# Regrouping the modulation pieces and retiming selection rounds and compressed attention in a fused two-block transformer kernel

## The chip, the cores and the metric

One core of a Trainium2 chip runs the whole program. The metric is the device time of one execution in microseconds (us). The kernel computes in float32: each weight tile and each activation is split into a high and a low part, and a product is three matmuls.

## The reference, cut to what matters

```python
mod = c @ w_ada[l] + b_ada[l]                     # 6 x 1024 values
h = rms_norm(x, g_pre_mix[l]) * (1.0 + sc1) + sh1 # uses the first two of six
proj = h @ w_in[l]
# nsa_attention: three branches of the same queries
k_cmp = compress(kc, ...); v_cmp = compress(vc, ...)   # a small MLP over blocks of 32 keys
o = g0 * o_cmp + g1 * o_slc + g2 * o_win
# dsa_attention
score = sum_h w_idx * relu(q_idx @ k_idx)         # per query, causal
_, sel = lax.top_k(score, 128)                    # keys that attention may see
```

The output projection, a gated residual, a squared-relu feed-forward and a second block (two SwiGLU layers around a mixer) follow. They take most of the time, and the change does not touch them.

## The kernel before

T = 512 tokens, D = 1024. Activations lie feature-major, 128 features by 512 tokens in a tile. The program writes out five instruction streams by hand (TensorE, ScalarE, VectorE, GpSimd and the DMA queue of SyncE, called SP below), and semaphores order them. Nothing is scheduled by a planner: what stands behind a waiting instruction of a stream waits too.

**Tile loop, n = 0 to 15.** Each n projects one tile of `w_in` (24 matmuls in 8 groups of 3, lines 342 to 344) into bank n % 2 (bank 0 from n = `WIDE` = 9). ScalarE copies it out (`projected`, L1087). SP then issues four small copies that swap the rotary halves (`turn_halves`, L2061), and VectorE (`rope`), later GpSimd, rotates it. Weights come through a ring of 4 slots in the order of `STREAM`: w_in 0 to 9, three tiles `cmp1k`, w_in 10 and 11, three tiles `cmp1v`, w_in 12 to 15, then w_out. `tile_load(i)` (L2041) waits until the tile 4 places earlier has been used. ScalarE (L1009) and VectorE (L1419) make its two parts.

**Late pieces.** The four late sixths of `mod` are summed from 16 loads `ada_late` of 1 MB each through two buffers. `late_load(i)` (L2035) waits until piece i-2 has been multiplied; `late_piece(i)` (L404, 8 matmuls) waits for the landing of its load. Pieces 0 to 15 are multiplied in tiles 0 to 3 and 5 to 8, one after the 4th group of the tile and one at its end. At n = 4, `ada_cols(1)` turns the first eight, and VectorE's `mod_cols(1)` (L1429) must read bank 7 before piece 8 may write it. The last of them is turned at pair 0 (`ada_cols(2)`).

**Index scores.** For n = 3 to 8 TensorE makes two index logits (L443), ScalarE applies relu (L1080), and VectorE sums them to three score tiles of 256, 384 and 512 keys. `top_round(r)` (L1533, L1534) takes the 8 greatest of a tile; there are 3 x 16 rounds, all due before pair 32.

**Compression.** `compress(0)` (L453, 64 recorded matmuls with `cmp1k`) runs at the end of n = 7 and `compress(1)` at pair 0. The ring slots of `w_in` 11 and of the `cmp1v` tiles are those of `cmp1k` 0 to 2 and `w_in` 10, so SP's loads of them wait for `compress(0)`.

**Pairs, p = 0 to 47.** A pair is a tile t of queries with two heads of one branch. From n = 9 on four pairs go with a tile, one after every second group; pairs 28 to 47 run alone. For pair p, TensorE does `qk(p)` (L478), then `turn_probs(p-2)` (L494) and `pv(p-3)` (L510). VectorE does `masked(p)` (L1586, twice), then `scaled(p-1)`, then rounds. ScalarE does two exponentials of pair p (L1117), then copies the turned probabilities of p-2 (L1104).

**Compressed branch.** `cmp_keys` at p = 6 makes keys and values (TensorE; nine copies of VectorE, L1570 and L1573). For i = 0 to 3 with p = `CMP_AT[i]`: `cmp_scores` at p, `cmp_turn` into bank 4 at p + 2, `cmp_out` at p + 4. At p + 2 ScalarE copies the turned block from bank 4 (L1125), behind the exponentials of that pair; TensorE's next `turn_probs` with a tile t of 2 or 3 needs bank 4 back, while t of 0 or 1 uses bank 4 + p % 2. The order of t in eight pairs is 3, 0, 2, 1, 3, 0, 2, 1. `outputs(n)` (L1109, L1608) reads a finished head pair at p = `OUT_AT[n]`.

SP's order for n = 0 to 7, where `pieces` is {0: 2, 1: 4, 2: 6, 3: 8, 5: 10, 6: 12, 7: 14}:

```python
for n in range(16):
    if n in pieces:
        late_load(pieces[n])
    if n != VC:                # VC = 4
        turn_halves(n)
    if n in pieces:
        late_load(pieces[n] + 1)
    while n in after and i <= place[after[n]]:
        tile_load(i)           # after[7] is the last cmp1v tile
        i += 1
```

Of the kernel before, what the change touches and what calls it, by code (L numbers as in the profile page):

```python
# [12 lines left out]
ACT = mybir.ActivationFunctionType  # L13
# [122 lines left out]
def build(nc, xt, consts, cols, pos, ada, ada_late, mats, extra, out):  # L136
    ctx = ExitStack()
    with ctx:
        sems = {}

        def S(name):
            if name not in sems:
                sems[name] = ctx.enter_context(nc.semaphore(name))
            return sems[name]
# [147 lines left out]
        steps = [(hh, c) for hh in range(HEADS) for c in (3, 2, 1, 0)]  # L292
        SLOTS = 14
        WIDE = 9
        CMP_AT = [9, 12, 18, 26]
        OUT_AT = [14, 19, 27, 35, 39, 43, 47, NP]
        slot_steps = [list(range(3 * n, min(3 * n + 3, 32))) for n in range(SLOTS)]

        NORMS = ["pre1", "post1", "f1", "post2", "g1", "mix", "g2"]
# [11 lines left out]
        def _(pe):  # L311
# [96 lines left out]
            def ada_cols(q):  # L408

                pe.wait_ge(S("ada_rows"), q + 1)  # L410
                claim(7, "mod", q + 1)
                for m in range(4):
                    mm = pe.matmul(bank[:, 7, m:16:4], ada_rows[:, m * P:(m + 1) * P], const("ident")[:, 0:P:32],
                                   start=True, stop=True)
                mm.then_inc(S("ada_cols"), 1)

            def late_piece(i):

                q, k = i // KD, i % KD
                pe.wait_ge(S(f"ada_in{i % 4}"), 16 * (i // 4 + 3))  # L420
                if k == 0:
                    claim(7, "ada_rows", q + 2)
                ada_sums(k, ada_late_in[i % 2], range(4)).then_inc(S("ada_sums"), 1)
# [117 lines left out]
            def pair_step(p):  # L541

                if p < NP:
                    qk(p)
                if p == 0:
                    ada_cols(2)
                    compress(1)
                if p == 6:
                    cmp_keys()
                if p in CMP_AT:  # L550
                    if p == CMP_AT[0]:
                        pe.wait_ge(S("cmp_kv"), 1)
                    cmp_scores(CMP_AT.index(p))
                if p - 2 in CMP_AT:
                    cmp_turn(CMP_AT.index(p - 2))
                if p - 4 in CMP_AT:
                    cmp_out(CMP_AT.index(p - 4))
                if 2 <= p < NP + 2:
                    turn_probs(p - 2)
                if 3 <= p:  # L560
                    pv(p - 3)

            for n in range(16):
                b = n % 2 if n < WIDE else 0
                claim(b, "ropein", n + 1)
                w = take("w_in", P, "proj_full", n + 1)
                for k in range(KD):
                    mm = product(bank[:, b, :], [v[:, k, :] for v in w], [hs[:, part, k, :] for part in (0, 1)],
                                 k == 0, k == KD - 1)
                    if k == KD - 1:  # L570
                        mm.then_inc(S("proj_full"), 1)
                    if n >= WIDE and k % 2 == 1:
                        pair_step(4 * (n - WIDE) + k // 2)
                    if n == 4 and k == KD - 1:
                        ada_cols(1)
                    elif n < WIDE and n != 4 and k in (3, KD - 1):
                        late_piece(2 * (n - (n > 4)) + k // 4)
                if 3 <= n < WIDE:
                    logits(2 * (n - 3))
                    logits(2 * (n - 3) + 1)  # L580
                if n == 7:
                    compress(0)
# [401 lines left out]
        def _(act):  # L984
# [120 lines left out]
                           .then_inc(S("probT"), 1)  # L1105

            def outputs(n):
                act.wait_ge(S("pv"), 11 if n == 0 else LAST_PAIR[n] + 1)
                act.activation(out_at(0, n), bank[:, 6 + (n + 1) % 2, :], ACT.Copy).then_inc(S("oT_hi"), 1)  # L1109

            def pair_step(p):
                t, br, i = pairs[p]
                kv = (t + 1) * P
                for e in range(2):
                    n = 2 * (p % 2) + e
                    act.wait_ge(S("smin"), 2 * p + e + 1)
                    act.activation(soft[p % 4][:, e, 0:kv], soft[p % 4][:, e, 0:kv], ACT.Exp, scale=-1.0,  # L1117
                                   bias=smin[:, n:n + 1], accum_out=ssum[:, n:n + 1]).then_inc(S("probs"), 1)
                if p in CMP_AT:
                    act.wait_ge(S("cmp_shift"), CMP_AT.index(p) + 1)  # L1120
                    act.activation(cs[:, 1, :, :], cs[:, 0, :, :], ACT.Exp, scale=-1.0).then_inc(S("cmp_exp"), 1)
                    own("cmp_exp")
                if p - 2 in CMP_AT:
                    act.wait_ge(S("cmp_turned"), CMP_AT.index(p - 2) + 1)
                    act.activation(cpt.rearrange("p a b -> p (a b)"), bank[:, 4, 0:256], ACT.Copy)\  # L1125
                       .then_inc(S("cmp_probT"), 1)
                if p >= 2:
                    probs_turned(p - 2)
                if p == 2:
                    act.wait_ge(S("cmp_hid"), 2)  # L1130
                    act.activation(hidc[:, :, :, :].rearrange("p m g n -> p (m g n)"), bank[:, 6, 0:4 * CMP_N],
                                   ACT.Gelu_apprx_tanh).then_inc(S("cmp_gelu"), 1)
                    log_exp_tables()
                if p in OUT_AT:
                    outputs(OUT_AT.index(p))

# [256 lines left out]
        def _(dve):  # L1393
# [149 lines left out]
            for n in range(WIDE):  # L1543
                if n >= 1:
                    rope(n - 1)
                if n == 5:
                    mod_cols(1)
                ahead("w_in", n, ("w_in", 15))
                if 3 <= n:
                    index_score(2 * (n - 3))  # L1550
                    index_score(2 * (n - 3) + 1)
                while n >= 5 and rounds < 4 * (n - 4):
                    top_round(rounds)
                    rounds += 1

# [71 lines left out]
            def cmp_probs(i):  # L1627
                c1 = cs[:, 1, :, :]
                c4 = c1.rearrange("p (e t) n -> p e t n", e=2)
                dve.wait_ge(S("cmp_exp"), i + 1)  # L1630
                do(dve.tensor_reduce(cmin[:, :], c1, AX.X, ALU.add))
                do(dve.reciprocal(coef[:, :], cmin[:, :]))
                gate = gates.rearrange("p t (h c) -> p h t c", c=3)[:, i:HEADS:4, :, 0]
                do(dve.tensor_tensor(coef2.rearrange("p (e t) -> p e t", e=2), coef.rearrange("p (e t) -> p e t", e=2), gate,
                                     ALU.mult))
                do(dve.tensor_tensor(c4, c4, by_tile(const("cmp_keep")), ALU.mult))
                dve.tensor_tensor(c1, c1, coef2[:, :, None].to_broadcast([P, HEADS, CMP_N]), ALU.mult)\
                   .then_inc(S("cmp_probs"), 1)
                own("cmp_probs")

            for p in range(NP + 1):
                if p < NP:
                    masked(p, 0)
                    masked(p, 1)
                    if p == 0:
                        late_mods()
                    if p == 6:
                        cmp_keys()
                    if p in CMP_AT:
                        cmp_masked(CMP_AT.index(p))  # L1650
                    if p - 1 in CMP_AT:
                        cmp_probs(CMP_AT.index(p - 1))
                if p >= 1:
                    scaled(p - 1)
                if p in OUT_AT[:-1]:
                    outputs(OUT_AT.index(p))
                if p % 4 == 1 and p // 4 + WIDE < 16:
                    lo(PINDEX["w_in", min(p // 4 + WIDE + 2, 15)])
                if p == 41:
                    lo(PINDEX["w_out", 2])  # L1660

                while p < NP and rounds < min(3 * ROUNDS, ROUNDS + p + 1):
                    top_round(rounds)
                    rounds += 1
            outputs(2 * NT - 1)
# [363 lines left out]
        def _(sy):  # L2029
# [41 lines left out]
                tile_load(i)  # L2071
                i += 1
            for n in range(16):
                if n in pieces:
                    late_load(pieces[n])
                if n != VC:
                    turn_halves(n)
                if n in pieces:
                    late_load(pieces[n] + 1)
                while n in after and i <= place[after[n]]:  # L2080
                    tile_load(i)
                    i += 1
            while i < len(STREAM):
                tile_load(i)
                i += 1
# [92 lines left out]
```

## Time and profile before

| what | value |
|---|---|
| three runs | 2030.14, 2030.39, 2032.83 us; median 2030.39 |
| profiled execution | 2032.83 us, span 2030.7 us |
| TensorE busy | 1876.2 us, 92% |
| VectorE, ScalarE, GpSimd busy | 44%, 34%, 10% |
| mean granted TensorE clock | 0.97 of full speed |
| tiles 0 to 8 | up to 154.5 us |
| tiles 9 to 15 with pairs 0 to 27 | 154.5 to about 290 us |
| pairs 28 to 47 alone | about 290 to 360.5 us |

The profiled execution is the longest of the three runs, 2.4 us above the median. Times inside the kernel are counted from the start of the span. A granted clock of 1.00 is 2.4 GHz, and 0.50 is 1.2 GHz.

### The profile page before, as it was taken

How to read it: one execution, taken by the hardware profiler on the slowest of the kernel's cores; microseconds unless marked ns; L12 is line 12 of the kernel's file. 1: busy time of each engine (PE TensorE's matmuls, PEld its weight loads, DVE VectorE, ACT ScalarE, POOL GpSimd, SP SyncE). 2: the span in 40 equal slices, each digit the busy share in tenths (PEclk: the TensorE clock that was granted, in tenths of full speed). 3: DMA queues.
4: the chain of work that ended last, by engine and by line, in shares of the span. 5: the costliest groups of instructions: out<-in, count | busy, mean ns of one | idle time of the engine just before them, and what ended most of it. 6: DMA issues, size and time to landing. Idle time of an engine off the chain costs nothing. (4 is left out here: it accounts for less than half of the span.)

```text
span 2030.7 us, 27890 instructions
## 1 busy us (share of the span) xinstructions
PE 1876.2 (92%) x11708; PEld 1445.0 (71%) x11708; DVE 891.1 (44%) x1446; ACT 692.4 (34%) x1127; POOL 203.0 (10%) x165
## 2 busy tenths in 40 slices
PE   5999988989999998999999988999498899999999
PEld 2666655758888885888888866666288578888887
DVE  5266866364434345333333342333755543332332
ACT  3215546242323233332223243545522333222321
POOL 0023434200000001000000200333100020000000
PEclk9999989989999998999999998999799999999999
DMA  9672100212222321233223212111000123322231
GB/s 370 217 256 80 39 20 32 73 52 94 94 93 97 98 97 52 94 105 102 75 103 120 69 64 78 44 42 32 0 4 4 33 83 104 109 90 92 94 123 43
DMA packets 44477, 176.17 MB, mean 87 GB/s; under 512 B 5568, under 2 KB 5824, under 8 KB 41024
## 3 DMA queue, kind: packets, MB, share of 16 engines
q1 hardware_dynamic: 44352, 174.38, 25.2%
q8 instruction: 93, 1.52, 0.3%
q14 instruction: 32, 0.26, 0.0%
HBM read 168.33 MB, written 2.10 MB: 84 GB/s over the span
## 5 line engine op out<-in xcount | busy, mean ns | idle before, releaser
L342 PE MATMUL bank<-hs,wsp 128*128 128x512 f32 x1368 | 549.7, 402 | 21.2 <-DVE hs L1458 11.5
L1009 ACT ACTIVATE wsp<-ring 128x1024 fp32r<-128x1024 f32 (+2 forms) x244 | 268.7, 1104 | 853.2 <-PE bank L344 851.5
L343 PE MATMUL bank<-hs,wsp 128*128 128x512 f32 x1368 | 538.8, 394 | 0.0
L344 PE MATMUL bank<-hs,wsp 128*128 128x512 f32 x1368 | 538.3, 393 | 0.0
L1419 DVE TENSOR_TENSOR wsp<-ring,wsp 128x1024 fp32r<-128x1024 f32 (+2 forms) x244 | 312.1, 1281 | 406.4 <-ACT wsp L1009 406.3
L342 PEld LDWEIGHTS bank<-hs,wsp 128*128 128x128 f32 x1368 | 260.7, 191 | 103.9 <-issue 42.1
L344 PEld LDWEIGHTS bank<-hs,wsp 128*128 128x128 f32 x1368 | 260.5, 190 | 55.8
L343 PEld LDWEIGHTS bank<-hs,wsp 128*128 128x128 f32 x1368 | 260.7, 191 | 54.3 <-issue 1.9
L344 PE MATMUL bank<-hids,wsp 128*128 128x512 f32 x608 | 241.0, 396 | 0.0
L343 PE MATMUL bank<-hids,wsp 128*128 128x512 f32 x608 | 241.0, 396 | 0.0
L342 PE MATMUL bank<-hids,wsp 128*128 128x512 f32 x608 | 241.0, 396 | 0.0
L1969 POOL TENSOR_TENSOR arena<-arena 128x512 f32<-128x512 f32 x24 | 43.2, 1802 | 981.0 <-ACT arena L1021 981.0
L344 PEld LDWEIGHTS bank<-hids,wsp 128*128 128x128 f32 x608 | 114.5, 188 | 27.9
L343 PEld LDWEIGHTS bank<-hids,wsp 128*128 128x128 f32 x608 | 114.5, 188 | 27.9
L342 PEld LDWEIGHTS bank<-hids,wsp 128*128 128x128 f32 x608 | 114.5, 188 | 27.9
L1723 DVE SCALAR_TENSOR_TENSOR x<-bank,x 128x512 f32<-128x512 f32 x40 | 27.7, 691 | 173.9 <-PE bank L344 173.9
L1713 DVE TENSOR_TENSOR tmp<-tmp,bank 128x512 f32<-128x512 f32 x44 | 30.2, 687 | 128.9 <-PE bank L344 128.9
L1117 ACT ACTIVATE arena<-arena,smin 128x512 f32<-128x512 f32 (+3 forms) x96 | 53.1, 554 | 75.4 <-DVE smin L1586 75.4
L494 PE MATMUL bank<-cst,arena 128*128 128x128 f32 x240 | 40.1, 299 | 25.7 <-ACT arena L1125 10.7
L494 PEld LDWEIGHTS bank<-cst,arena 128*128 128x128 f32 x240 | 27.3, 148 | 43.9 <-ACT tmp L1104 13.5
L1675 DVE TENSOR_TENSOR arena<-arena,bank 128x512 f32<-128x512 f32 x24 | 16.5, 688 | 73.8 <-PE bank L344 73.8
L404 PE MATMUL bank<-arena,c 128*32 128x512 f32 x176 | 26.5, 686 | 24.0 <-DMA arena<-ada 15.2
(305 smaller groups left out, 1934.3 us busy)
## 6 DMA issues: line engine op xcount, KB each, us to landing
ring<-m_gate SPq DMA_DIRECT2D x44, 512.0 KB, 3.4
ring<-m_up SPq DMA_DIRECT2D x44, 512.0 KB, 3.4
ring<-m_down SPq DMA_DIRECT2D x32, 704.0 KB, 4.1
ring<-m_w_in SPq DMA_DIRECT2D x38, 512.0 KB, 3.5
arena<-ada_late SPq DMA_DIRECT2D x16, 1024.0 KB, 6.5
ring<-m_w_up SPq DMA_DIRECT2D x32, 512.0 KB, 3.4
ring<-m_w_down SPq DMA_DIRECT2D x32, 512.0 KB, 3.4
ring<-m_w_out SPq DMA_DIRECT2D x16, 512.0 KB, 3.6
```

The source lines that it names most:

```text
L342: pe.matmul(out, lhs[0], rhs[0], start=start, stop=False)
L343: pe.matmul(out, lhs[0], rhs[1], start=False, stop=False)
L344: return pe.matmul(out, lhs[1], rhs[0], start=False, stop=stop)
L404: mm = pe.matmul(bank[32 * j:32 * j + 32, 7, :], c32[:, k, :], tile[:, n * T:(n + 1) * T], start=(k == 0), stop=(k == KD - 1), skip_group_ ...
L494: mm = pe.transpose(bank[:, b, (c + k) * P:(c + k + 1) * P], soft[p % 4][:, e, k * P:(k + 1) * P], const("ident"))
L1009: act.activation(wsp[:, s % SPLIT, 0, 0:size], ring[:, i % RING, 0:size], ACT.Copy)\
L1117: act.activation(soft[p % 4][:, e, 0:kv], soft[p % 4][:, e, 0:kv], ACT.Exp, scale=-1.0, bias=smin[:, n:n + 1], accum_out=ssum[:, n:n + 1]) ...
L1419: dve.tensor_tensor(wsp[:, s % SPLIT, 1, 0:size], ring[:, i % RING, 0:size], wsp[:, s % SPLIT, 0, 0:size].bitcast(F32), ALU.subtract).then ...
L1675: ins = dve.tensor_tensor(ybuf[:, nn, :], ybuf[:, nn, :], bank[:, nn % 4, :], ALU.add)
L1713: dve.tensor_tensor(f, f, bank[:, 2 * (nn % 2) + 1, :], ALU.mult).then_inc(S("gated"), 1)
L1723: dve.scalar_tensor_tensor(out=x[:, nn, :], in0=bank[:, nn % 4, :], scalar=scale, in1=x[:, nn, :], op0=ALU.mult, op1=ALU.add).then_inc(S(" ...
L1969: pool.tensor_tensor(sq[:, 0, :], sq[:, 0, :], sq[:, k, :], ALU.add).then_inc(S("sq_sum"), 1)
```

## The change

Six edits:

1. TensorE multiplies both late pieces of a tile at its end, one behind the other.
2. SP issues the two late loads of a tile behind the rotary copies and behind the ring loads of that tile.
3. VectorE does 2 selection rounds for each of the tiles 5 to 8 in place of 4; in the pairs the total after pair p is 8 + 5(p+1)//4 in place of 16 + p + 1. Both reach 48 at pair 31.
4. `cmp_keys` moves from pair 6 to pair 4.
5. `CMP_AT` goes from 9, 12, 18, 26 to 7, 10, 18, 26, and `OUT_AT[0]` from 14 to 12.
6. The copy of the turned block from bank 4 moves from ScalarE to VectorE, behind `masked` of the pair and ahead of `scaled`.

```diff
-        CMP_AT = [9, 12, 18, 26]
-        OUT_AT = [14, 19, 27, 35, 39, 43, 47, NP]
+        CMP_AT = [7, 10, 18, 26]
+        OUT_AT = [12, 19, 27, 35, 39, 43, 47, NP]
 # TensorE (cmp_keys moves to p == 4 on VectorE too)
-                if p == 6:
+                if p == 4:
                     cmp_keys()
-                    if n == 4 and k == KD - 1:
-                        ada_cols(1)
-                    elif n < WIDE and n != 4 and k in (3, KD - 1):
-                        late_piece(2 * (n - (n > 4)) + k // 4)
+                if n < 4:
+                    late_piece(2 * n)
+                    late_piece(2 * n + 1)
+                elif n == 4:
+                    ada_cols(1)
+                elif n < WIDE:
+                    late_piece(2 * n - 2)
+                    late_piece(2 * n - 1)
 # ScalarE
-                act.wait_ge(S("pv"), 11 if n == 0 else LAST_PAIR[n] + 1)
+                act.wait_ge(S("pv"), 9 if n == 0 else LAST_PAIR[n] + 1)
-                if p - 2 in CMP_AT:
-                    act.wait_ge(S("cmp_turned"), CMP_AT.index(p - 2) + 1)
-                    act.activation(cpt.rearrange("p a b -> p (a b)"), bank[:, 4, 0:256], ACT.Copy)\
-                       .then_inc(S("cmp_probT"), 1)
 # VectorE
-                while n >= 5 and rounds < 4 * (n - 4):
+                while n >= 5 and rounds < 2 * (n - 4):
+                    if p - 2 in CMP_AT:
+                        dve.wait_ge(S("cmp_turned"), CMP_AT.index(p - 2) + 1)
+                        dve.tensor_copy(cpt.rearrange("p a b -> p (a b)"), bank[:, 4, 0:256]).then_inc(S("cmp_probT"), 1)
+                        own("cmp_probT")
-                while p < NP and rounds < min(3 * ROUNDS, ROUNDS + p + 1):
+                while p < NP and rounds < min(3 * ROUNDS, 2 * (WIDE - 5) + 5 * (p + 1) // 4):
 # SP
-                if n in pieces:
-                    late_load(pieces[n])
                 if n != VC:
                     turn_halves(n)
-                if n in pieces:
-                    late_load(pieces[n] + 1)
                 while n in after and i <= place[after[n]]:
                     tile_load(i)
                     i += 1
+                if n in pieces:
+                    late_load(pieces[n])
+                    late_load(pieces[n] + 1)
```

## Rows read from the trace of the kernel before

**Rows 1.** The profile's page: busy time of each engine.

```profile
PE 1876.2 (92%) x11708; PEld 1445.0 (71%) x11708; DVE 891.1 (44%) x1446; ACT 692.4 (34%) x1127; POOL 203.0 (10%) x165
```

**Rows 2.** TensorE's waits from 50 to 360 us: total, times, longest.

```profile
PE bank L494 <- ACT arena L1125: 10.7, 3, 4.8
...
PE bank L404 <- DMA arena<-ada_late: 4.9, 3, 4.4
PE bank L404 <- DVE mod L1429: 3.9, 1, 3.9
...
PE bank L494 <- DVEq L1575: 1.9, 1, 1.9
```

**Rows 3.** Stretches: length, TensorE busy (instructions), granted clock, DMA share, GB/s.

```profile
73.40:80.20 6.80, 5.63 (x17) 0.50 0.95 348
...
114.30:117.70 3.40, 3.40 (x9) 0.50 0.72 243
```

**Rows 4.** Timeline of TensorE: start, length, line, and the idle time before it.

```profile
74.56 1.93 PE L404 MATMUL bank<-arena,c 128*32 128x512 f32 x8 [4.43 <-DMA arena<-ada_late]
...
148.46 1.07 PE L404 MATMUL bank<-arena,c 128*32 128x512 f32 x8
...
152.41 1.06 PE L404 MATMUL bank<-arena,c 128*32 128x512 f32 x8
153.40 1.13 PE L443 MATMUL bank<-arena 64*128 64x512 f32 x4
154.46 0.50 PE L342 MATMUL bank<-hs,wsp 128*128 128x512 f32 x1
...
257.55 1.45 PE L494 MATMUL bank<-cst,arena 128*128 128x128 f32 x6 [3.51 <-ACT arena L1125]
...
312.07 0.93 PE L494 MATMUL bank<-cst,arena 128*128 128x128 f32 x4 [1.82 <-ACT tmp L1104]
```

**Rows 5.** Line 453 from 138 to 146 us: `compress(0)`, with first and last start.

```profile
L453 PE MATMUL bank<-arena,ring x64: 275/275/323, 138.3 to 145.4; 128*128 128x64 f32 x64
```

**Rows 6.** Timeline of SP's queue: start and length of the issues.

```profile
133.47 0.33 SPq L2035 DMA_DIRECT2D arena<-ada_late  x1
...
145.74 0.33 SPq L2041 DMA_DIRECT2D ring<-m_w_in  x1
146.11 1.94 SPq L2041 DMA_DIRECT2D ring<-m_cmp1v  x3
153.14 2.41 SPq L2061 DMA_DIRECT2D tmp<-tmp  x4
155.62 0.55 SPq L2041 DMA_DIRECT2D ring<-m_w_in  x1
```

**Rows 7.** The late load issued at 114.12 us, alone on the queue: time to landing.

```profile
DMA to landing us min/median/max: 4.8/4.8/4.8
```

**Rows 8.** The w_in load issued at 92.86 us: time to landing.

```profile
DMA to landing us min/median/max: 5.7/5.7/5.7
```

**Rows 9.** The late load issued behind it at 94.52 us: time to landing.

```profile
DMA to landing us min/median/max: 6.9/6.9/6.9
```

**Rows 10.** The w_in load issued at 145.74 us: time to landing.

```profile
DMA to landing us min/median/max: 3.5/3.5/3.5
```

**Rows 11.** The three cmp1v loads issued from 146.11 to 147.72 us: time to landing.

```profile
DMA to landing us min/median/max: 4.9/6.3/7.2
```

**Rows 12.** Timeline of VectorE: its copies for `cmp_keys`; round ahead of `masked(20)`.

```profile
187.34 2.00 DVE L1573 COPY arena<-bank 32x64 f32<-32x64 f32 x8
...
253.47 0.68 DVE L1533 MAX8 best<-arena 128x8 f32<-128x512 f32 x1
...
254.98 0.69 DVE L1586 CUSTOM_DVE_ANT_0 arena<-bank,cst 128x512 f32<-128x512 f32 x1
...
256.20 0.08 DVE L1586 DVE_READ_ACCUMULATOR2_ANT smin<- 128x1 f32 x1
```

**Rows 13.** Timeline of ScalarE: the copy that TensorE waited for at 257.55 us.

```profile
257.14 0.36 ACT L1125 ACTIVATE arena<-bank 128x256 f32<-128x256 f32 x1
```

More of the change, by code:

```diff
@@ L1646, in _ @@
                         late_mods()
-                    if p == 6:
+                    if p == 4:
                         cmp_keys()
```

## The prediction, made before the change was run

> **What bounds the kernel now.** I read the page first: TensorE is busy 92% of the span, no other engine over half [rows 1]. So an edit is worth what it does to TensorE's idle time or clock. The edits lie between tile 0 and pair 47, and from 360 us on the program is unchanged. The table of TensorE's waits up to there names three kinds that the edits touch: 4.9 us for late loads, 3.9 us for `mod_cols(1)`, and 10.7 us in three waits for the bank 4 copy; one more, of 1.9 us, is for the copies of `cmp_keys` [rows 2]. The clock comes next: after the 4.4 us wait for piece 2 TensorE was granted 0.50, that is 1.2 GHz, for 6.8 us, and after the wait for mod for 3.4 us [rows 3]. Half speed for 3.4 us of dense matmuls loses 1.7 us. Eight matmuls of a piece took 1.93 us at that level and 1.07 us at the other [rows 4]. Last I read the timelines, for what each stream would reach first in the new order.
>
> **Edits 1 and 2: both pieces at the tile's end, their loads behind everything else.** The work on TensorE is the same, so only waits and clock count. The steps, from the rows: from one piece's start to the next is 3.95 us, of which a piece is 1.0, so half a tile is 2.95 and a tile 5.9 [rows 4]. SP's first rotary copy follows the tile's end by 0.7 us (152.41 to 153.14), and the load behind the four copies follows that by 2.5 (155.62) [rows 4, 6]. A w_in load on a quiet queue lands 3.5 us after issue, a late load 4.8 [rows 10, 7]. One behind another, the late load landed at 101.4 and the w_in load ahead of it at 98.6: 2.8 us more per MB [rows 8, 9]. I take 1.4 for half an MB. The pair of late loads for the next tile is then ready at E + 0.7 + 2.5 + 3.5 + 2.8 = E + 9.5 and E + 12.3, where E is the end of this tile's matmuls. TensorE without waits wants them at E + 8 (two pieces 2.05, tile 5.9) and E + 9. The pair is late wherever the queue starts fresh.
>
> Tile by tile. TensorE reached piece 2 at 70.1 (74.56 less 4.43), half a tile short of the end [rows 4], so E1 = 73.1. Piece 2 landed at 74.5 without a w_in load ahead of it; with it, at 76.0, and piece 3 at 78.8: waits of 2.9 and 1.8, next tile at 79.8. E2 = 85.7; these loads had been queued during the waits and land in time (83.7, 86.5). Pieces end 87.8, E3 = 93.7, and pieces 6 and 7 are ready at E2 + 9.5 = 95.2 and 98.0: waits 1.5 and 1.8. Two logits (0.65) bring 99.7. E4 = 105.6, then columns and logits 1.6, E5 = 113.1. Pieces 8 and 9 have landed by then. The bank 7 wait: VectorE read `mod` just ahead of 113.0, and its logits come 0.7 later now, so 0 to 0.6 us stays of the 3.9; I take 0. Next tile at 116.0, E6 = 121.9. Here a cmp1k load of 704 KB is ahead, 4.0 by the bounds 3.5 and 4.8: ready at 123.1 and 125.9, waits 1.2 and 1.8, next tile 127.8. E7 = 133.7, loads in time again, 136.8 after the logits.
>
> Now the main term. `compress(0)` takes 7.2 us [rows 5] and ends at 144.0. Before, piece 14 was issued at 133.47 [rows 6] and piece 15 behind the rotary copies of tile 7, both ahead of the loads that wait for `compress(0)`. Now SP stands at w_in 11 until 144.0 and both late loads stand behind it. SP then issues w_in 11, three cmp1v loads and only then pieces 14 and 15. The last cmp1v load landed at 147.72 + 7.2 = 154.9, which is 9.2 after the w_in issue at 145.74 [rows 6, 11]. Two more MB make 12.0 and 14.8: pieces 14 and 15 are ready at 156.0 and 158.8. E8 is 149.9: a wait of 6.1, then 1.8. They end at 159.9 and the logits at 161.0. Before, tile 9 began at 154.46 [rows 4]. **6.5 us later**, though the 4.4 and 3.9 us waits and the two falls of the clock have gone out of the sum.
>
> The Trainium skill (DMA: Bandwidth & Descriptors, Anatomy of one DMA) says that DMA engines never wait on a semaphore, the wait stands on the issuing sequencer ahead of dispatch; by that rule the blocked w_in load holds back two loads that have nothing to wait for. It also fits a load of the other issue path as 2.0 us plus bytes over 436 GB/s, an estimate of 4.4 us for 1 MB where the row shows 4.8; the six loads would be done by it in 13.0 us and not 14.8, and the sum would be 1.8 lower.
>
> **Clock.** New falls have to be added. A fall followed each of the two long waits in these tiles [rows 3]; the new waits are eight, seven of them shorter than those. Bounds: none (0), or two levels of 3.4 us at tiles 1 and 8 and one each at 3 and 6 (10 us). I take a long one behind the 6.1 us wait (3.4) and a short one elsewhere (1.7): 5.
>
> **Edit 3: rounds.** A 512-wide round is 1.5 us (253.47 to 254.98) [rows 12]. The 8 rounds taken out of tiles 5 to 8 lie where TensorE waits for loads; they hide nothing, except at n = 8, where pair 0 starts sooner on VectorE. TensorE is at `compress(1)` then, so that is worth 0. They come back as a second round at pairs 3, 7, 11, ... 31, each just ahead of `masked` of a pair with t = 3. At pair 31 VectorE had no idle time, and TensorE's 1.82 us wait at 312.07 is for ScalarE behind `masked(32)` [rows 4]: +1.5. The others cost 0 to 0.5 each; I take 0.5 together.
>
> **Edits 5 and 6: the bank 4 copy.** `masked(20)` ended at 256.28, the two exponentials and the copy at 257.50, TensorE went on at 257.55 [rows 12, 13, 4]. With the copy behind `masked` on VectorE (0.4 from ScalarE's 0.36) TensorE would go on at 256.75, 0.8 earlier. But pair 19 now has two rounds: +1.5, net +0.7. Pair 28 is the same with its extra round at 27: +0.7. The wait at pair 14 moves to 12, with a double round at 11 too: from -1 to +1, I take -0.5. The copy makes `scaled`, queued behind it, 0.4 later, which GpSimd waits for: up to 0.4 each, I take 0.3 in all. Bounds of the term: -3 to +4.
>
> **Edit 4: `cmp_keys` at 4.** The copies (2.0 us) [rows 12] now run behind a `masked` pair 0.25 longer; the wait of 1.9 us stays at 1.9 to 2.3: +0.3.
>
> **Sum.** 6.5 + 5 + 1.5 + 0.5 + 0.7 + 0.7 - 0.5 + 0.3 + 0.3 = 15.0. The profiled execution has span 2030.7 and 2.1 us around it: 2045.7 and 2047.8. It ran 2.4 above the median of 2030.39, so the median becomes 2045.4; I say 2045.
>
> **Rivals.**
> *A cheap wait at tile 8* (0.16). Slower, but little: no new fall of the clock, loads at the faster rate, tail neutral. 6.5 - 2 + 0: 2034 to 2037. For it: two short waits with a piece between them are not one long one. Against: rows 3.
> *Nothing to see* (0.06). The pieces wait less because each pair lands inside the tile, leaving only 8 us at tile 8 against 8.3 us of removed waits and 3.4 to 4 us of clock, about 2030 with the clock lost once. Against: the DMA share is already 0.95 and 0.72 in the rows at the first tiles [rows 3], so later issue cannot be caught up.
> *The bank 4 copy pays* (0.08, other side). If VectorE is free when TensorE has turned the block, the three waits of 10.7 us [rows 2] shrink to about 3 and the falls behind them (about 4 us) go: -12, against +6.5 and a short fall: 2027. It decides once VectorE reaches the copy 2.5 us or more before ScalarE did. Against: on VectorE's timeline the round ran straight into `masked(20)` with no idle time.
> The forecast case, 8 to 24 us slower, has 0.70; its own range is 2038 to 2054.
>
> About 0.2%, 4 us, is the least that a measurement of this kernel tells from no change. Slower 0.86, same 0.07, faster 0.07. Range: from the cheap case, 2034, to all falls and the tail's bound, 6.5 + 10 + 7, 2054.
>
> **What would show it.** TensorE's waits for ada_late rise from 4.9 to about 18, the longest 6 us before piece 14; SP issues pieces 14 and 15 behind three cmp1v loads; the wait for mod is under 1; tile 9 begins at 161 to 166; the bank 4 waits stay near 10 us, now ended by VectorE; pairs 28 to 47 take 1 to 3 us more. Wrong would be: SP issuing piece 14 ahead of 144 us, or the waits at bank 4 under 5 us.

## The result, and the profile after

| | median | lowest to highest |
|---|---|---|
| before | 2031.61 us | 2030.14 to 2036.73 (4 runs) |
| changed | 2057.34 us | 2053.63 to 2057.83 (4 runs) |

The ratio is 1.0125, with a 95% interval of 1.0108 to 1.0140: about 26 us slower. The forecast was 15 us slower, 2034 to 2054 us. The direction held; the size did not, and the time lies 3 us outside the range.

The profiled execution of the changed kernel took 2059.2 us, 1.9 above the median; its span is 2057.1 us, 26.4 more than before. Tile 9 began at 170.60 where it had begun at 154.46: 16.1 us. From there to the first matmul of `w_out` it took 214.6 us (170.60 to 385.25) in place of 206.0: 8.6 us. The rest, unchanged work, took 1671.9 in place of 1670.2 us. The three parts, 16.1, 8.6 and 1.6, are all of it. The last cannot be put down to the change: in the fourteen profiles of this document the same work took 1667.8 to 1672.1 us.

TensorE's waits from 50 to 400 us in the changed kernel: total, times, longest.

```profile
PE bank L404 <- DMA arena<-ada_late: 21.6, 8, 6.0
PE bank L494 <- DVE arena L1655: 11.7, 3, 5.5
...
PE bank L494 <- DVE arena L1618: 3.7, 4, 1.6
PE bank L494 <- DVEq L1575: 2.3, 1, 2.3
...
PE bank L478 <- DVE smin L1586: 1.6, 1, 1.6
```

The wait for `mod` is gone. The waits for late loads went from 4.9 to 21.6 us. The three bank 4 waits are now ended by VectorE's copy (L1655) and are 11.7 us where they were 10.7 [rows 2]. The last row is new: `qk(33)` waits for `masked(32)`.

SP's queue around `compress(0)` in the changed kernel, beside [rows 6]:

```profile
130.68 3.70 SPq L2039 DMA_DIRECT2D arena<-ada_late  x2
142.47 2.41 SPq L2065 DMA_DIRECT2D tmp<-tmp  x4
152.04 0.33 SPq L2045 DMA_DIRECT2D ring<-m_w_in  x1
152.42 1.42 SPq L2045 DMA_DIRECT2D ring<-m_cmp1v  x3
153.89 1.20 SPq L2039 DMA_DIRECT2D arena<-ada_late  x2
```

Nothing is issued from 144.9 to 152.04. Then w_in 11 and three cmp1v loads go first, and pieces 14 and 15 last. TensorE's timeline of the same kernel shows what that costs:

```profile
76.21 1.94 PE L404 MATMUL bank<-arena,c 128*32 128x512 f32 x8 [4.72 <-DMA arena<-ada_late]
79.90 1.94 PE L404 MATMUL bank<-arena,c 128*32 128x512 f32 x8 [1.76 <-DMA arena<-ada_late]
...
163.56 1.08 PE L404 MATMUL bank<-arena,c 128*32 128x512 f32 x4 [6.01 <-DMA arena<-ada_late]
...
166.73 1.94 PE L404 MATMUL bank<-arena,c 128*32 128x512 f32 x8 [1.23 <-DMA arena<-ada_late]
168.59 2.08 PE L443 MATMUL bank<-arena 64*128 64x512 f32 x4
170.60 0.63 PE L342 MATMUL bank<-hs,wsp 128*128 128x512 f32 x1
```

The 6.01 us before piece 14 is the wait that was foreseen. Also to be seen is the length of a piece, 1.94 us where [rows 4] show 1.06, and of the logits, 2.08 in place of 1.13. Stretches of the changed kernel (from and to, length, busy time of TensorE, its weight loads, VectorE, ScalarE and GpSimd, then granted clock, DMA share, GB/s):

```profile
75.30:85.50 10.20, 7.54 (x25) 3.40 (x26) 1.39 (x2) 0.00 (x0) 0.00 (x0) 0.50 0.93 312
...
99.20:106.00 6.80, 5.11 (x21) 1.20 (x14) 0.74 (x2) 0.49 (x2) 0.00 (x0) 0.50 0.96 333
...
129.90:136.70 6.80, 4.74 (x19) 1.72 (x16) 0.66 (x2) 0.87 (x2) 0.00 (x0) 0.50 0.96 342
...
160.70:170.90 10.20, 6.11 (x21) 1.21 (x22) 0.00 (x0) 0.20 (x1) 0.00 (x0) 0.50 0.68 255
```

A fall to 1.2 GHz goes with each of the four pairs of waits, 34 us in all, where [rows 3] show 6.8 and 3.4 us. All four began before the second wait of the pair did. At tiles 1 and 8 the low clock began while TensorE still stood in the first wait (75.3 and 160.7, waits over at 76.21 and 163.56). At tiles 3 and 6 it began at 99.2 and 129.9, 0.3 and 1.0 us after the first wait had ended; the second waits began at 100.7 and 130.0.

From tile 9 to `w_out`, first in the kernel before, then in the changed kernel (columns as above):

```profile
154.46:360.48 206.02, 176.43 (x1311) 117.43 (x1309) 144.87 (x468) 111.28 (x301) 78.18 (x72) 0.95 0.13 39
```

```profile
170.60:385.25 214.65, 179.79 (x1311) 119.71 (x1309) 151.50 (x489) 110.32 (x297) 78.11 (x71) 0.93 0.11 34
```

Length less busy time is TensorE's idle time: 29.6 us before, 34.9 after.

VectorE's timeline ahead of pair 20 in the changed kernel, beside [rows 12]:

```profile
274.77 0.55 DVE L1533 MAX8 best<-arena 128x8 f32<-128x384 f32 x1
...
276.41 0.69 DVE L1533 MAX8 best<-arena 128x8 f32<-128x512 f32 x1
...
277.93 0.69 DVE L1586 CUSTOM_DVE_ANT_0 arena<-bank,cst 128x512 f32<-128x512 f32 x1
...
279.15 0.42 DVE L1655 COPY arena<-bank 128x256 f32<-128x256 f32 x1
```

Two rounds and the closing compare of a tile stand between `outputs(1)` and `masked(20)`: 3.2 us, where one round took 1.5. The copy follows `masked` at once and TensorE goes on at 279.63, after 4.29 us in place of 3.51 [rows 4].

### The profile page after: what moved, and what is told of

Its sections match the earlier page's. It is cut to its first block and busy times, and to the rows that moved or that the text cites. A ratio compares the mean times of both kernels' runs of the same rounds, so it can differ in the third digit from the quotient of the medians.

```text
span 2057.1 us, 27890 instructions
## 1 busy us (share of the span) xinstructions
PE 1886.6 (92%) x11708; PEld 1451.0 (71%) x11708; DVE 889.8 (43%) x1450; ACT 691.5 (34%) x1123; POOL 202.3 (10%) x165
## 5 line engine op out<-in xcount | busy, mean ns | idle before, releaser
L342 PE MATMUL bank<-hs,wsp 128*128 128x512 f32 x1368 | 549.7, 402 | 22.5 <-DVE hs L1458 11.5
L494 PE MATMUL bank<-cst,arena 128*128 128x128 f32 x240 | 41.1, 304 | 29.4 <-DVE arena L1655 11.7
L404 PE MATMUL bank<-arena,c 128*32 128x512 f32 x176 | 30.8, 802 | 36.9 <-DMA arena<-ada_late 21.6
L494 PEld LDWEIGHTS bank<-cst,arena 128*128 128x128 f32 x240 | 27.8, 151 | 47.6 <-ACT tmp L1108 13.7
```

The costliest lines, as they stand in the source:

```text
L342: pe.matmul(out, lhs[0], rhs[0], start=start, stop=False)
L404: mm = pe.matmul(bank[32 * j:32 * j + 32, 7, :], c32[:, k, :], tile[:, n * T:(n + 1) * T], start=(k == 0), stop=(k == KD - 1), skip_group_ ...
L494: mm = pe.transpose(bank[:, b, (c + k) * P:(c + k + 1) * P], soft[p % 4][:, e, k * P:(k + 1) * P], const("ident"))
```

## The experiments

Theory: edits 1 and 2 make the late loads late and drop the clock behind each wait, and edit 3 puts a second round ahead of `masked` where TensorE waits for it. Rivals: the parts only hurt together; the clock is hidden in the waits; 8 more rounds on VectorE cost wherever they stand; the moved copy costs by itself. Ratios are to the kernel before, run beside each. A gain or a loss in us is the ratio less 1, times the time of the kernel before, unless medians are named; the two can differ by some us.

**1. Edits 1 and 2 alone.** Both as in the diff of the change.

> The kernel before with edits 1 and 2 alone (late pieces in pairs at the tile's end, their loads behind the ring loads). My theory, the late loads and the clock that falls behind their waits: about two thirds of the loss is here, 14 to 19 us over the kernel before (tile 9 began 16.1 us later in the changed kernel's profile), TensorE's waits for late loads near 21 us. Rival, the moved rounds and the compressed branch on VectorE are the cause: under 8 us.

Measured: 2051.45 us beside 2033.53, ratio 1.0103 (1.0072 to 1.0135), 21 us. TensorE's waits:

```profile
PE bank L404 <- DMA arena<-ada_late: 23.2, 8, 6.4
```

The theory holds. The ratio puts the loss 2 us above its range, the medians (18 us) inside it; the four runs lie in two groups, two at 2048 us and two at 2055 and 2057. This half is seven to eight tenths of the loss.

**2. Edits 3 to 6 alone.**

> Edits 3 to 6 alone (rounds, cmp_keys, CMP_AT, copy on VectorE), late pieces as before. My theory: the remaining third, 4 to 11 us over the kernel before, because a second round stands ahead of masked at pairs 12, 20, 28 and 32; in the tiles 0 to 8 nothing is lost or up to 2 us are won. Rival, the two halves of the change only hurt together: within 2 us of the kernel before.

Measured: 2041.38 us, ratio 1.0043 (1.0030 to 1.0057), 9 us, in the expected range. The halves sum to 1.0146, at or a little above the whole, 1.0125 (1.0108 to 1.0140). They do not need each other.

**3. The late loads of tile 7 ahead of the blocked ring loads.** Edits 1 and 2, and on SP:

```diff
                 if n != VC:
                     turn_halves(n)
+                if n == 7:
+                    late_load(pieces[n])
+                    late_load(pieces[n] + 1)
                 while n in after and i <= place[after[n]]:
                     tile_load(i)
                     i += 1
-                if n in pieces:
+                if n in pieces and n != 7:
```

> Edits 1 and 2, but the two late loads of tile 7 are issued ahead of the ring loads that wait for compress(0). My theory: the 6 us wait before piece 14 and the clock fall behind it go, so 8 to 11 us less than edits 1 and 2 as they are. Rival, the queue is full anyway and the wait comes back at piece 15 or at the next w_in tile: under 4 us less.

Measured: 2042.17 us, ratio 1.0050 (1.0026 to 1.0075), 11 us below experiment 1 by the ratios and 9 by the medians; the two intervals barely overlap. SP's queue and TensorE's waits in this kernel:

```profile
142.06 1.07 SPq L2039 DMA_DIRECT2D arena<-ada_late  x2
149.16 0.33 SPq L2045 DMA_DIRECT2D ring<-m_w_in  x1
```

```profile
PE bank L404 <- DMA arena<-ada_late: 13.5, 6, 2.8
```

The 6 us wait is gone and no wait came in its place. Two loads moved past one waiting instruction are about half of what edits 1 and 2 cost.

**4. Edit 1 alone.**

> Edit 1 alone: pieces in pairs at the tile's end on TensorE, SP's order as before. My theory, the place of the loads on SP's queue is what costs: within 5 us of the kernel before, because the first load of each pair is issued ahead of the rotary copies and none stands behind compress(0). Rival, pairing the pieces is what costs, since the first buffer is given back half a tile later: 8 us or more over the kernel before.

Measured: 2032.15 us, ratio 1.0003 (0.9985 to 1.0020). TensorE's waits:

```profile
PE bank L404 <- DMA arena<-ada_late: 7.9, 5, 2.3
...
PE bank L404 <- DVE mod L1433: 1.2, 1, 1.2
```

Pairing the pieces is free. The wait for `mod` shrinks and the late loads take back about as much.

**5. Edits 1 and 2 with TensorE kept busy in the waits.** The extra matmuls write a bank nobody reads.

```diff
+        FILL = {1: 4, 3: 2, 6: 2, 8: 6}
+                if n in FILL:
+                    for _ in range(FILL[n]):
+                        pe.matmul(bank[:, 5, :], const("ones"), x[:, 0, :], start=True, stop=True)
...
+                    late_piece(2 * n - 2)
+                    if n in FILL:
+                        for _ in range(2):
+                            pe.matmul(bank[:, 5, :], const("ones"), x[:, 0, :], start=True, stop=True)
+                    late_piece(2 * n - 1)
```

> Edits 1 and 2, with extra matmuls into the unused bank 5 where TensorE waits for late loads: ahead of the first piece of tiles 1, 3, 6 and 8 (4, 2, 2 and 6 of 512 columns) and 2 between the two pieces of those tiles. They add work that the result does not use. My theory, a good part of the loss is the clock that falls behind the waits: TensorE is granted 1.2 GHz for under 15 us up to tile 9 in place of 30.7, and the kernel is 4 to 10 us faster than edits 1 and 2 as they are. Rival, the chain of loads alone sets these tiles and the low clock is hidden in the waits: within 3 us of edits 1 and 2, or slower by the added work.

Measured: 2044.68 us, ratio 1.0045 (1.0022 to 1.0068), against 1.0103 for experiment 1. The stretches from just ahead of piece 0 to tile 9, first this kernel, then experiment 1 (columns as above):

```profile
63.80:166.10 102.30, 95.31 (x467) 57.04 (x465) 47.09 (x82) 19.68 (x30) 13.17 (x9) 1.00 0.70 248
```

```profile
64.00:173.70 109.70, 86.49 (x425) 52.84 (x423) 45.48 (x82) 20.20 (x30) 12.06 (x9) 0.86 0.64 231
```

With the clock at 1.00 throughout, tile 9 began at 166.1 in place of 173.6, 7.6 us sooner, though TensorE was busy 8.8 us more. All eight pieces still waited for their loads (7.0 us in all, where it was 23.2), so the extra matmuls held none of them back. The rival, that the low clock hides in the waits, has fallen. What the loads alone cost is the rest: tile 9 at 166.1 against 154.5 in the kernel before, which itself had 10 us of low clock there.

**6. Edit 3 alone.**

> Edit 3 alone: 8 rounds less up to tile 8, a second round at every fourth pair. My theory, this is the larger part of what edits 3 to 6 cost: 4 to 8 us over the kernel before, the three waits for the bank 4 copy at about 14 us in sum (10.7 before, plus 1.2 at pair 14 not at all, 1.5 at 20 and 28 each). Rival, the cost is in the copy and the moved pairs: within 2 us of the kernel before.

Measured: 2040.65 us, ratio 1.0041 (1.0027 to 1.0054), 8 us: about all of what edits 3 to 6 cost. TensorE's waits:

```profile
PE bank L494 <- ACT arena L1125: 13.9, 3, 6.3
```

**7. Edits 4 to 6 alone.**

> Edits 4, 5 and 6 alone, rounds as before. My theory, the copy on VectorE is 0.8 us sooner at pairs 20 and 28: bank 4 waits near 8 to 9 us, time within 3 us of the kernel before. Rival, the move itself costs: 4 us or more slower.

Measured: 2036.67 us, ratio 1.0008 (0.9991 to 1.0024). TensorE's waits:

```profile
PE bank L494 <- DVE arena L1651: 8.0, 3, 4.0
```

The moved copy shortens these waits by 2.7 us, as worked out; no gain is seen in the time. The profile shows why there need be none: TensorE's idle time from tile 9 to `w_out` is 29.5 us where it was 29.6. Other waits took the gain back, among them those for `cmp_masked` (3.0 to 3.9 us). The moved pairs (edits 4 and 5) were not run without the copy, nor the copy without them or without a change of the rounds.

**8. The copy on VectorE, and no round ahead of pairs 14, 20 and 28.**

```diff
-                while p < NP and rounds < min(3 * ROUNDS, ROUNDS + p + 1):
+                while p < NP and rounds < min(3 * ROUNDS, ROUNDS + p + (p - 1 not in CMP_AT[1:])):
```

> Edit 6 alone, and the round of pairs 13, 19 and 27 done one pair later, so that none stands ahead of masked at pairs 14, 20 and 28. If the round ahead of masked is what TensorE waits for, the three bank 4 waits fall from 10.7 to under 6 us and the kernel is 3 to 8 us faster than before. Rival, the waits are set by the exponentials or by TensorE itself: 9 us or more stay.

Measured: 2022.43 us beside 2033.87, ratio 0.9945 (0.9927 to 0.9963), 11 us faster than before, more than expected. TensorE's waits:

```profile
PE bank L494 <- DVE arena L1651: 4.9, 3, 2.4
```

**9. Edit 3 with the second round at pairs 2, 6, 10, ... 30.**

```diff
-rounds < min(3 * ROUNDS, 2 * (WIDE - 5) + 5 * (p + 1) // 4)
+rounds < min(3 * ROUNDS, 2 * (WIDE - 5) + p + 1 + (p + 2) // 4)
```

> Edit 3, but the second round of every four pairs stands at pairs 2, 6, 10, ... 30, ahead of a one- or two-tile pair, and not at 3, 7, 11, ... 31, ahead of a four-tile pair. If the place of the second round is what costs, this lies 4 us or more below edit 3 alone and within 4 us of the kernel before, the bank 4 waits at 10.7 us. If 8 more rounds on VectorE cost wherever they stand, it lies with edit 3 alone, 6 to 10 us over the kernel before.

Measured: 2036.4 us beside 2035.3, ratio 1.0009 (0.9995 to 1.0023). TensorE's waits:

```profile
PE bank L494 <- ACT arena L1125: 11.4, 3, 4.8
```

The same rounds one pair earlier cost nothing that can be measured, 6 us less than in experiment 6, so it is their place more than their number. The profiles are less clear than the times: TensorE's idle time from tile 9 to `w_out` is 36.1 us in experiment 6, 32.9 here and 29.6 before. Of this kernel's 30.7 us of low clock in that stretch, 13.7 us go with no wait (Open, below).

**10. The skipped rounds alone, the copy on ScalarE.**

> Only the rounds of pairs 13, 19 and 27 done one pair later; the copy stays on ScalarE. The three bank 4 waits were 10.7 us before and 4.9 with the copy on VectorE too. If both parts add, I expect 6.5 to 8 here and the kernel 4 to 8 us faster than before; if the round is all, 5 and 9 to 12 us faster.

Measured: 2030.58 us beside 2035.3, ratio 0.9980 (0.9968 to 0.9992), 4 us faster. TensorE's waits:

```profile
PE bank L494 <- ACT arena L1125: 7.4, 3, 3.3
```

The waits fall from 10.7 by 3.3 for the rounds and by 2.5 more, to 4.9, with the copy: in the waits both parts add. In the time the copy is worth about 7 us here (experiment 8 against this one), more than its 2.5 us of waits. The profiles have 10.2 and 17.1 us of low clock between tile 9 and `w_out`, which may be a part of it; that was not tested.

**11. Edit 2 alone.**

> Edit 2 alone: loads of both pieces behind rotary copies and ring loads, pieces on TensorE half a tile apart as before. My theory, the place of the loads costs by itself: waits for late loads of 20 us or more (the first piece is wanted half a tile sooner), 15 to 30 us over the kernel before. Rival, only pairing and place together cost: under 5 us over it.

Measured: 2078.55 us, ratio 1.0207 (1.0191 to 1.0224), 42 us slower, beyond the expected 30. TensorE's waits:

```profile
PE bank L404 <- DMA arena<-ada_late: 35.6, 6, 8.7
```

So in the change edit 1 repairs half of what edit 2 does.

**12. The best version: edit 1, the copy on VectorE, the skipped rounds.**

> Edit 1 with SP's order as before, the copy on VectorE, and the rounds of pairs 13, 19 and 27 one pair later. The profiles say that edit 1 shortens the wait for mod from 3.9 to 1.2 us. If that adds to the later gain, 11 to 17 us faster than before; if the clock or the loads eat it, 8 to 11 us, as without edit 1.

Measured: 2020.14 us (2019.41 to 2024.66) beside 2035.3, ratio 0.9931 (0.9918 to 0.9944), 14 us faster than before and 37 us faster by the medians than the change, which was not run beside it. TensorE's waits:

```profile
PE bank L404 <- DMA arena<-ada_late: 6.3, 5, 2.1
PE bank L494 <- DVE arena L1655: 4.9, 3, 2.4
...
PE bank L404 <- DVE mod L1429: 2.1, 1, 2.1
```

More than half of its interval lies within that of experiment 8 (0.9927 to 0.9963), so whether edit 1 adds anything is not settled.

## Why the prediction was wrong in size

**Direction and places: right.** The four pairs of waits stood at tiles 1, 3, 6 and 8, none at 2 and 7, and the longest was 6.0 us where 6.1 was worked out. The wait for `mod` went. Piece 14 was issued behind the cmp1v loads. Moving those two loads alone gave back about 10 us (experiment 3). By the Trainium skill's rule (DMA: Bandwidth & Descriptors, Anatomy of one DMA), that the wait stands on the issuing sequencer and not on the DMA engines, the trace agrees: SP issued nothing from 144.9 to 152.04 and everything within 3 us after.

**The step that failed is "Clock."** It took one long and one short fall, 5 us, with the reason that seven of the eight new waits are shorter than the two in rows 3; the upper bound allowed 10 us with falls at all four places. The measured falls came at all four: 10.2, 6.8, 6.8 and 10.2 us. Filling the waits (experiment 5) won 7.6 us at tile 9, and the ratio fell from 1.0103 to 1.0045. So the term was about 7.5 and not 5, and short waits had been priced too low. At tiles 3 and 6 a first wait of 2.1 and 2.0 us was enough. The trace of the kernel before shows it too, past tile 9 and outside [rows 3]: TensorE went on at 189.45 after a wait of 1.87 us, and the clock was low from 189.4 to 192.8 (columns of the second row as in [rows 3]).

```profile
189.45 1.11 PE L494 MATMUL bank<-cst,arena 128*128 128x128 f32 x4 [1.87 <-DVEq L1575]
```

```profile
189.40:192.80 3.40, 3.35 (x15) 0.50 0.00 0
```

The 1.82 us wait of [rows 4] at 312.07 also has a fall behind it, from 312.3 to 315.7. Not every such wait has: none stands behind 2.03 us at 176.2 or 2.40 us at 228.2. The pairs of waits are surer. In the profiles of the changed kernel and of experiments 1, 3 and 4, two waits of 1.7 to 2.8 us with one piece between them stand at eight places, and a fall goes with each.

The other side of the same error is that the forecast treated the low clock as a term added at the end. It sits in the chain: tile 2 took 7.4 us in place of 5.9 and piece 3 took 1.9 in place of 1.1. The tile's end came at 89.2 instead of 85.7 (0.9 of these 3.5 us is the load step, next), and the next loads, issued from there, were late by as much.

**The step between the two loads of a pair was too small.** It was taken as 2.8 us per MB from rows 8 and 9. The second piece started 3.69, 3.43, 3.13 and 3.17 us after the first: about 0.5 us more in each of four pairs, 2 us. With that and the clock, tile 9 came 9.6 us later than the forecast's own 161.0; 5 of these 9.6 had been put in as clock, so 4.6 us of the miss lie here.

**The tail: 3.5 forecast, 8.6 measured.** The bank 4 term was right: 10.7 + 0.7 + 0.7 - 0.5 = 11.6, measured 11.7. The term for the round at pair 31 was right in size: a new wait of 1.6. All idle time in the tail grew by 5.3 us, from 29.6 to 34.9. Missed in it were small waits elsewhere: `cmp_masked` 3.0 to 3.7, and one of 1.2 for ScalarE's probabilities, which experiment 3's profile has as well, with the tail of the kernel before. The other 3.3 us are clock, for which the forecast had no term in the tail: 30.7 us of it were low where the kernel before has 20.5. How much of that the change causes is not shown. Six profiles with the tail of the kernel before (itself and experiments 1, 3, 4, 5 and 11) have 13.7 to 23.9 us of low clock there, and experiment 2, with the tail of the changed kernel, has 23.9. No step had the wrong sign.

**The range.** Its upper end was 6.5 + 10 for tile 9 and 7 for the tail. Tile 9 came 16.1 us later, inside its bound; the tail's 8.6 and the 1.6 of the unchanged work carried the time out of the range.

**The rivals.** The cheap wait at tile 8 and "nothing to see" are out: falls came at all four places, and the waits for late loads are 21.6 us. One of the two rows given against the second as "at the first tiles" is not of them: 114.30 to 117.70 lies in tile 5. The copy on VectorE does pay, as the third rival had it, once no round stands ahead of `masked`: waits of 8.0 with the old rounds, 4.9 without, and 11 us in the time where the rival had 12 for it. It named as its condition that VectorE reaches the copy 2.5 us or more before ScalarE did. In experiment 8 the three waits are 1.3, 2.2 and 2.4 us shorter, so a little less was enough; edit 3 moved it the other way. The edits as given cancel what edit 6 wins.

**Open.** Why a fall lasts 3.4, 6.8 or 10.2 us was not tried, nor why one wait of 2 us has a fall behind it and the next has none. The low clock differs between profiles of the same work, and it may be what spreads the time of one kernel: before ran from 2026 to 2042 us in the runs beside the experiments. Nor are waits all of it. In the profiles of experiments 9 and 12 the clock fell inside `compress(1)` and stayed low for 13.7 us, with TensorE busy throughout and no wait above 0.3 us in the 20 us before. In experiment 9 the 64 matmuls of `compress(1)` took 11.5 us, against 7.3 in the kernel before; the low stretch is this row (columns as in the rows of experiment 5):

```profile
158.60:172.20 13.60, 13.60 (x55) 12.07 (x55) 3.74 (x17) 2.40 (x8) 0.44 (x1) 0.50 0.26 94
```

## What to carry to other kernels

On a queue that executes in order, ask of each issue you move what the instruction now ahead of it waits for; two loads put behind one wait cost about 10 us here, and the loads had nothing to wait for themselves. Where two engines hand over every few microseconds, put optional work behind a hand-over that has slack: the same rounds cost 8 us ahead of a four-tile pair and nothing one pair earlier, and taking three rounds away from there, with the copy, won 11 us. When you price the clock, do not pass over waits of 2 us: two with a short burst between them had a fall at eight places of eight here, and of the four single ones named above two had. Put the low clock into the chain, not at its end.

## What the runs showed of the hardware that was not expected

Matmuls whose result nobody reads paid for themselves: 22 of them into an unused bank, in the waits, kept the granted clock at 1.00 from piece 0 to tile 9, 102 us, where it had been 0.86. They made the kernel 7 us faster by the medians (2044.68 against 2051.45), with TensorE 8.8 us busier in that stretch.

The clock also fell with no wait to go with it: 13.7 us at 1.2 GHz, begun among 64 matmuls of 64 columns (experiments 9 and 12) that ran at full clock in the kernel before.
